# A decode step with expert retrieval: the sample's memory products moved ahead of tile 1's scores, and tile 1's values behind the sample's queries

## The reference

```
xn      = rms_norm(x, g_mix)
q,k,v,gu,gv = split(xn @ w_in)                  # 512, 128, 128, 512, 512 columns
attn    = sink_attention(rope(q), rope(k), v)   # window 128; 8 query heads, 2 key heads
sgu     = gelu(gu) * (tril(w_s) @ rms_norm(gelu(gv)) + b_s)   # per chunk of 128 tokens
x      += concat(rms_norm(attn), rms_norm(sgu)) @ w_out
x      += softmax(q_c @ mem_k / 8) @ mem_v @ w_co,  q_c = rms_norm(x, g_cross) @ w_cq
# experts, for each token and each of 8 heads:
s1, i1  = top_k(q1 @ sub_keys1, 16);  s2, i2 = top_k(q2 @ sub_keys2, 16)
top,sel = top_k(s1[:,None] + s2[None,:], 16);   gate = softmax(top)
idx     = i1*128 + i2 at sel                     # of 16384 experts
x      += sum_k gelu(xn . u_tab[idx_k]) * gate_k * v_tab[idx_k],  xn = rms_norm(x, g_ffn)
y       = rms_norm(x, g_final)
```

## Time and profile before

| | us |
|---|---|
| three runs: median (lowest, highest) | 1709.17 (1706.82, 1710.81) |
| the profiled execution: its own time | 1707.81 |
| its span, first to last instruction | 1706.0 |
| TensorE busy | 1301.5 (76%) |
| VectorE busy | 1165.7 (68%) |
| ScalarE busy | 810.4 (48%) |
| GpSimd busy | 641.3 (38%) |
| data moved | 657.35 MB, mean 385 GB/s |

### The profile page before, as it was taken

How to read it: one execution, slowest core, us unless ns; L and a number is a source line. 1 busy time by engine, 2 the same in 40 slices (tenths; PEclk the granted TensorE clock), 3 DMA queues, 4 the chain that set the end, 5 groups by cost and what they waited for, 6 DMA issues and landing times.

```text
span 1706.0 us, 21619 instructions
## 1 busy us (share of the span) xinstructions
PE 1301.5 (76%) x7069; PEld 475.1 (28%) x7069; DVE 1165.7 (68%) x2795; ACT 810.4 (48%) x2337; POOL 641.3 (38%) x584
## 2 busy tenths in 40 slices
PE   9999878987889776677777776776767677667665
PEld 4455523433444222122322111111111111111110
DVE  2544578887667677787777777777667677677764
ACT  1434366775444354455555454445444445444443
POOL 0000044434434344444444443444444444444441
PEclk9999998899999988899988777878888877888866
DMA  9433699999999999999999999999999999999995
GB/s 353 168 138 134 232 400 422 408 374 422 421 421 421 420 398 420 421 403 421 419 421 412 422 421 421 421 422 421 421 421 421 421 405 422 421 421 420 422 419 220
DMA packets 99041, 657.35 MB, mean 385 GB/s; under 512 B 12576, under 2 KB 17568, under 8 KB 22368
## 3 DMA queue, kind: packets, MB, share of 16 engines
q0 software_dynamic: 83056, 604.28, 85.7%
q1 hardware_dynamic: 15872, 51.68, 8.1%
HBM read 652.71 MB, written 4.19 MB: 385 GB/s over the span
## 4 chain that ended last, share of the span: by engine, by line
DMA 44%; PE 26%; ACT 11%; DVE 10%; issue 7%; POOL 2%; ACTq 0%; DVEq 0%; SPq 0%; POOLq 0%
DMA R<-in_peer_uv,R 43%; PE ps L2009 10%; PE ps L1543 6%; DVE R L1462 4%; PE ps L1802 3%; ACT L911 2%; ACT R L920 2%; PE ps L1515 2%; ACT R L915 1%; POOL R L641 1%; ACT R L911 1%; ACT L826 1%; DVE R L1285 1%; DVE R L1286 1%; DVE R L1288 1%
## 5 line engine op out<-in xcount | busy, mean ns | idle before, releaser
L2009 PE MATMUL ps<-R 64*64 64x512 f32 x4536 | 732.3, 725 | 370.4 <-ACT R L920 364.9
L641 POOL DMA_INDIRECT R<-in_peer_uv,R x567 | 627.8, 1107 | 966.4 <-PE ps L2009 762.8
L1462 DVE CUSTOM_DVE_ANT_0 R<-R 128x1024 f32<-128x1024 f32 x567 | 689.3, 1225 | 382.4 <-DMA R<-in_peer_uv,R 368.3
L911 ACT ACTIVATE R<-R 128x1 f32<-128x1 f32 x576 | 115.9, 201 | 594.6 <-DVE R L1462 585.2
L2009 PEld LDWEIGHTS ps<-R 64*64 64x64 f32 x4536 | 134.5, 149 | 713.3 <-ACT R L920 627.1
L920 ACT ACTIVATE R<-R 128x64 f32<-128x64 f32 x576 | 200.4, 348 | 54.3 <-ACT R L915 1.5
L1802 PE MATMUL ps<-A,R 128*128 128x256 f32 (+1 forms) x640 | 224.8, 479 | 0.7 <-ACT R L802 0.7
L915 ACT ACTIVATE R<-R 128x1 f32<-128x1 f32 x576 | 169.8, 295 | 21.2 <-ACT R L911 0.4
L1802 PEld LDWEIGHTS ps<-A,R 128*128 128x128 f32 (+1 forms) x640 | 96.3, 201 | 261.9 <-issue 260.4
L1543 PE MATMUL ps<-A,R 128*128 128x512 f32 (+1 forms) x256 | 101.1, 547 | 0.0
L911 ACT ACT_TABLE_LOAD x60 | 77.0, 1283 | 9.0 <-DVE R L1462 8.0
(11 more groups left out here) (288 smaller groups left out, 936.6 us busy)
## 6 DMA issues: line engine op xcount, KB each, us to landing
R<-in_peer_uv,R POOLq DMA_INDIRECT x567
A<-in_w_pq SPq DMA_DIRECT2D x8, 1024.0 KB, 10.3
A<-in_w_in SPq DMA_DIRECT2D x3, 2048.0 KB, 20.5
R<-in_w_out SPq DMA_DIRECT2D x5, 1024.0 KB
x_res<-in_x_prompt SPq DMA_DIRECT2D x6, 512.0 KB, 12.9
R<-in_w_out SPq DMA_DIRECT2D x1, 3072.0 KB
R<-in_x_promptT SPq DMA_DIRECT2D x4, 512.0 KB, 9.2
R<-in_w_cq SPq DMA_DIRECT2D x2, 1024.0 KB, 10.9
```

What stands on the lines that cost most here:

```text
L641: pool.indirect_dma_start(slots[slot_of[g]], None, I["peer_uv"][:, :], bass.IndirectOffsetOnAxis(ap=idx[:, b % 4, k:k + 1], axis=0)).then_ ...
L911: act.activation(hgelu[:, b % 2, col], hdot[:, b % 2, col], ACT.Gelu).then_inc(gelu_ready, 1)
L1462: dve.tensor_tensor_reduce(u, u, xn(t), 1.0, 0.0, ALU.mult, ALU.add, hdot[:, b % 2, k:k + 1]).then_inc(u_used, 1)
L2009: ins = pe.matmul(bank(2 * (t % 2) + q)[rows], diag[tokens, g % DIAGS, :], v_rows[slot_of[g]][tokens, c * 512:(c + 1) * 512], start=first, ...
```

## The change

On TensorE's list the memory product (l_pv) moves ahead of tile 1's scores, and both stand after only 4 of the 16 instructions of tile 4's gates, whose rest follows in two pieces behind the fold and behind `half_T(3)`. The transposes of the sample's normed rows move ahead of `gating(4)`; tile 1's value product moves behind `q_mm(0)`, `half_T(4)` behind `scores(0)`, tile 1's transposes behind `q_mm(1)`. On ScalarE the copy of the fold goes ahead of tile 1's exponentials, the sample's norm ahead of tile 4's gates, and the square and root of tile 1's attention behind the sample's score copy. On VectorE tile 1's maxima go behind the sample's weighting, `half_take(3)` and `half_rows(4)` change places, `ffn(0)` signals xn_ready after the lower half (a new semaphore, xn_second, signals the upper one to the first dot product), `attn_scaled(1)` stands behind the first two key searches, and `half_take(4)` and `attn_take(1)` behind `best_pairs(0)`. In the expert loop tile 1's preparation, query, cross, FFN and the first two units start one expert later. Each moved piece keeps its waits, apart from one of VectorE for its own signal attn_out 2, which is left out. No arithmetic is added or removed.

```diff
@@ -351,7 +351,7 @@
...
 
-        xn_ready = sem("xn_ready")
+        xn_ready, xn_second = sem("xn_ready"), sem("xn_second")
         pq_q, pq_qo, pq_t, pq_to, pq_s, pq_so = (sem(n) for n in ("pq_q", "pq_qo", "pq_t", "pq_to", "pq_s", "pq_so"))
@@ -414,11 +414,11 @@
...
 
-        PREP_AT = {1: 1, 2: 122, 3: 200, 4: 210}
-        QUERY_AT = {1: 6, 2: 134, 3: 208, 4: 218}
-        CROSS_AT = {1: 9, 2: 138, 3: 222, 4: 244}
-        FFN_AT = {1: 28, 2: 158, 3: 268, 4: 16 * 23 + 2}
-        UNIT_AT = (24, 31, 38, 44, 51, 57)
+        PREP_AT = {1: 2, 2: 122, 3: 200, 4: 210}
+        QUERY_AT = {1: 7, 2: 134, 3: 208, 4: 218}
+        CROSS_AT = {1: 10, 2: 138, 3: 222, 4: 244}
+        FFN_AT = {1: 29, 2: 158, 3: 268, 4: 16 * 23 + 2}
+        UNIT_AT = (25, 32, 38, 44, 51, 57)
         OUT_AT = (77, 81, 85, 91, 95, 99, 105, 109, 113, 119, 123, 127)
@@ -784,27 +784,22 @@
...
             gating_std(4)
+            act.wait_ge(l_oT, 1)
+            act.activation(oT_c, v3(bank(5)[:, 0:P], 2), ACT.Copy).then_inc(l_oTo, 1)
             act.wait_ge(sc_max, 2)
...
             act.activation(es, es, ACT.Exp).then_inc(sc_exp, 1)
-            act.wait_ge(l_oT, 1)
-            act.activation(oT_c, v3(bank(5)[:, 0:P], 2), ACT.Copy).then_inc(l_oTo, 1)
+            act.wait_ge(x2_out, 1)
+            act.wait_ge(p_tr, 2)
+            row_norm(0, xn(0), f_std, ss_f)
             gates_out(4)
...
             act.activation(pT_one, v3(ps[:, 1024:2048], HEADS), ACT.Copy).then_inc(pT_out, 1)
-
-            act.wait_ge(x2_out, 1)
-            act.wait_ge(p_tr, 2)
-            row_norm(0, xn(0), f_std, ss_f)
             act.wait_ge(f_tr, 1)
...
             half_norm(4)
-            act.wait_ge(attn_out, 2)
-            chain(act.activation(pT_one.rearrange("p a b -> p (a b)")[:, 0:512], o_one, ACT.Square,
-                                 accum_out=ss_a[:, 1:2]))
-            act.activation(ss_a[:, 1:2], ss_a[:, 1:2], ACT.Sqrt, bias=eps[:, 0:1], scale=1.0 / 512).then_inc(n_std, 1)
 
@@ -830,6 +825,10 @@
...
             act.activation(mv_l, mv, ACT.Copy).then_inc(mv_moved, 1)
+            act.wait_ge(attn_out, 2)
+            chain(act.activation(pT_one.rearrange("p a b -> p (a b)")[:, 0:512], o_one, ACT.Square,
+                                 accum_out=ss_a[:, 1:2]))
+            act.activation(ss_a[:, 1:2], ss_a[:, 1:2], ACT.Sqrt, bias=eps[:, 0:1], scale=1.0 / 512).then_inc(n_std, 1)
             queries_out(1)
@@ -1223,13 +1222,6 @@
...
 
-            dve.wait_ge(sc_done, 2)
-            chain(dve.scalar_tensor_tensor(s_one, v3(ps[:, 0:1024], HEADS), 0.125,
-                                           band[:, P:2 * P].unsqueeze(1).broadcast_to([P, HEADS, P]), ALU.mult, ALU.add))
-            chain(dve.tensor_reduce(mx, s_one, AX_X, ALU.max))
-            chain(dve.tensor_tensor(mx, mx, sinks[:, :], ALU.max))
-            chain(dve.tensor_scalar(nmx, mx, -1.0, None, ALU.mult))
-            dve.tensor_tensor(es, nmx, sinks[:, :], ALU.add).then_inc(sc_max, 1)
             dve.wait_ge(l_exp, 1)
@@ -1238,8 +1230,14 @@
...
                               spread[:, 0:8].unsqueeze(2).broadcast_to([P, 8, HD]), ALU.mult).then_inc(l_o, 1)
+            dve.wait_ge(sc_done, 2)
+            chain(dve.scalar_tensor_tensor(s_one, v3(ps[:, 0:1024], HEADS), 0.125,
+                                           band[:, P:2 * P].unsqueeze(1).broadcast_to([P, HEADS, P]), ALU.mult, ALU.add))
+            chain(dve.tensor_reduce(mx, s_one, AX_X, ALU.max))
+            chain(dve.tensor_tensor(mx, mx, sinks[:, :], ALU.max))
+            chain(dve.tensor_scalar(nmx, mx, -1.0, None, ALU.mult))
+            dve.tensor_tensor(es, nmx, sinks[:, :], ALU.add).then_inc(sc_max, 1)
             gating_values(4)
-            half_take(3)
             add_halves(l_wo, x2_out)
@@ -1247,20 +1245,23 @@
...
                 chain(dve.reciprocal(rs_f[r, t:t + 1], ss_f[r, t:t + 1]))
-                for to in (LO, HI) if t == 0 else (ALL,):
-                    ins = dve.scalar_tensor_tensor(xn(t)[to], xr(t)[r], rs_f[r, t:t + 1], g_ffn[r], ALU.mult, ALU.mult)
-                ins.then_inc(xn_ready, 1)
+                dve.scalar_tensor_tensor(xn(t)[r], xr(t)[r], rs_f[r, t:t + 1], g_ffn[r], ALU.mult, ALU.mult)\
+                   .then_inc(xn_ready, 1)
+                if t == 0:
+                    dve.scalar_tensor_tensor(xn(0)[HI], xr(0)[r], rs_f[r, 0:1], g_ffn[r], ALU.mult, ALU.mult)\
+                       .then_inc(xn_second, 1)
 
...
             ffn(0)
+            half_take(3)
             gated(4)
+            half_rows(4)
             dve.wait_ge(pv_done, 2)
...
                               rden.unsqueeze(2).broadcast_to([P, HEADS, HD]), ALU.mult).then_inc(attn_out, 1)
-            half_rows(4)
 
@@ -1273,11 +1274,6 @@
...
                                   ALU.mult).then_inc(n_T, 1)
-
-            dve.wait_ge(attn_out, 2)
-            attn_scaled(1, o_one)
-            half_take(4)
-            attn_take(1)
 
@@ -1331,9 +1327,12 @@
...
                 top_keys(0, c)
+            attn_scaled(1, o_one)
             dve.wait_ge(mv_moved, 1)
...
             best_pairs(0)
+            half_take(4)
+            attn_take(1)
             experts_of(0, 0)
@@ -1453,6 +1452,7 @@
...
                     dve.wait_ge(xn_ready, t + 1)
+                    dve.wait_ge(xn_second, 1)
                 for k in range(TOPK):
@@ -1737,13 +1737,7 @@
...
             project(4, 1)
-            pe.wait_ge(q_out, TILES)
-            pe.wait_ge(kv_out, TILES)
-            for h in (0, 4, 1, 5, 2, 6, 3, 7):
-                rows = slice(64 * (h // 4), 64 * (h // 4) + 64)
-                ins = pe.matmul(ps[:, h * P:(h + 1) * P], qT_one[rows, h % 4, :], kT_of(1)[rows], start=True, stop=True)
-            ins.then_inc(sc_done, 1)
-            project(4, 2, 0, 4)
+            project(4, 2, 0, 2)
             pe.wait_ge(l_pTo, 1)
@@ -1753,19 +1747,25 @@
...
             ins.then_inc(l_pv, 1)
-            project(4, 2, 4, 6)
+            pe.wait_ge(q_out, TILES)
+            pe.wait_ge(kv_out, TILES)
+            for h in (0, 4, 1, 5, 2, 6, 3, 7):
+                rows = slice(64 * (h // 4), 64 * (h // 4) + 64)
+                ins = pe.matmul(ps[:, h * P:(h + 1) * P], qT_one[rows, h % 4, :], kT_of(1)[rows], start=True, stop=True)
+            ins.then_inc(sc_done, 1)
             pe.wait_ge(l_o, 1)
...
             ins.then_inc(l_oT, 1)
-            project(4, 2, 6, KD)
+            project(4, 2, 2, 4)
             pe.wait_ge(l_oTo, 1)
...
             half_T(3)
+            project(4, 2, 4, KD)
             pe.wait_ge(sgu_out, 4)
@@ -1774,15 +1774,10 @@
...
             ins.then_inc(pT_done, 1)
+            pe.wait_ge(xn_ready, 1)
+            sample_T(xn(0), f_tr, False)
             pe.wait_ge(qkT_out, 10)
             gating(4, bank(6))
-            pe.wait_ge(pT_out, 3)
-            for h in range(HEADS):
-                ins = pe.matmul(bank(0)[:, h * HD:(h + 1) * HD], pT_one[:, h, :],
-                                v_rows_of(1)[:, (h // 4) * HD:(h // 4 + 1) * HD], start=True, stop=True)
-            ins.then_inc(pv_done, 1)
-            pe.wait_ge(xn_ready, 1)
-            sample_T(xn(0), f_tr, False)
 
@@ -1832,14 +1827,19 @@
...
             q_mm(0)
-            half_T(4)
+            pe.wait_ge(pT_out, 3)
+            for h in range(HEADS):
+                ins = pe.matmul(bank(0)[:, h * HD:(h + 1) * HD], pT_one[:, h, :],
+                                v_rows_of(1)[:, (h // 4) * HD:(h // 4 + 1) * HD], start=True, stop=True)
+            ins.then_inc(pv_done, 1)
             pe.wait_ge(h_T, 3)
             q_T(0)
-            attn_T(1, o_one, bank(1))
             pe.wait_ge(sgu_out, TILES)
...
             scores(0)
+            half_T(4)
             q_mm(1)
+            attn_T(1, o_one, bank(1))
             pe.wait_ge(n_T, 1)
```

## The result

The changed kernel is slower: 1721.69 us (median of 6 runs, 1716.90 to 1723.17) against 1709.25 us (6 runs, 1706.72 to 1710.81), a ratio of 1.0074, 95% interval 1.0063 to 1.0086. That is 12.4 us where +1.3 was forecast, and above the range.

The account below looks back on a forecast made before the run. The stream of 576 expert gathers bounds the kernel, gated by the first index list and tile 1's output projection end. Projection +3.9, recovery -2.6, other shifts 0: +1.3 us, 1710.5 on the median; range 1704.0 to 1716.5.

Parts of the forecast that it names:

- The other shifts by one expert (query, cross, FFN, first two units) move equal work: 0, within 2 us either way: Expert loop: each ScalarE visit there carries two table loads of 1.28 us, so these shifts cost 0.
- the hole at 371: Gather stream, 371 to 376 us: 3.7 us lost behind the fifth query block's search, unchanged by the change: 0.
- The late projection: Tile 1's output projection waits for both takes, TensorE idles 3.8 us, end +3.9 us, bounds +0.8 and +5.6.
- real gain: Sample's query product on TensorE: idle time gone, takes 3.66 us instead of 6.63, ends 4.5 us earlier.
- the low clock in the projection: Tile 1's output projection: one stretch of 3.4 us at half speed, costing 1.7 us.
- Rival A: Late projection end not absorbed by the stream, clock low for two stretches: +5.6 us, 1714.8 us; chance 0.27.
- The memory wait: TensorE waits 3.8 us for the sample's memory values, whose product then takes 3.4 us; tile 1's exponentials end later.
- The recovery: Gather stream behind the fifth gather: preparation moved off the third expert and a partial refill win back 2.6 of 3.9 us.
- The index list: First index list, which opens the gather stream: ready at 204.85, 0.9 us earlier.
- The table loads: ScalarE table changes: only 1.28 us load, no drain; with the skill's 2.66 us the sum would be +2.7.
- g_ffn: Load for the sample's FFN norm: takes 4.4 us, lands at 180.25, now ends last by 0.5 us.

Follow-up runs that it names:

- e7: Kernel before with only the first two units one expert later (25, 32): 1714.44 us, ratio 1.0030.
- e3: Changed kernel with tile 1's scaling between the two key searches and both takes ahead of the best pairs: 1714.40 us, ratio 1.0034.
- e4: Changed kernel with the memory products behind tile 1's scores again, as before: 1720.30 us, ratio 1.0068.
- e9: Kernel of e5 with the memory products behind tile 1's scores again: 1714.47 us, ratio 1.0036.
- e6: Kernel before with tile 1's preparation, query, cross and FFN one expert later, units unmoved: 1706.93 us, ratio 0.9989.
- e5: Changed kernel with tile 1's scaling and both takes early as in e3, first two units back at 24 and 31: 1711.23 us, ratio 1.0013.
- e15: Kernel of e5 with tile 4's gates ahead of the sample's norm and its gating ahead of the sample's transposes, as before: 1715.56 us, ratio 1.0043.
- e8: Kernel of e6 with xn_ready signalled after the lower half of the scaled rows, no other reordering: 1707.53 us, ratio 0.9994.
- e2: Kernel before with the change's five expert-loop tables (preparation, query, cross, FFN, first two units one expert later): 1711.63 us, ratio 1.0025.
- e12: Kernel of e7 with unit 1's scaling, transposes and take one step earlier: 1712.08 us, ratio 1.0019.
- e13: Kernel before with all six units one expert later, distances between them kept: 1711.90 us, ratio 1.0030.
- e11: Kernel of e9 with tile 4's gates and the copies for the transposes ahead of the sample's norm on ScalarE: 1714.65 us, ratio 1.0035.

## Why the prediction was wrong, step by step

**The failed step is "The other shifts by one expert (query, cross, FFN, first two units) move equal work: 0, within 2 us either way".** The units' shift alone costs 5.1 us in the old order (e7, ratio 1.0030, 1.0017 to 1.0042). The work is equal; its place is not. TensorE at expert 50 waits for VectorE's work at expert 53 instead of 52, and while it stands there, no slot comes free. In the trace of before this wait was visible, 1.81 us at L1971 at 349.27, and the prediction did not look for it: it read the hole at 371 and took the stretch before it as full. The FFN's shift is of the same kind (2.06 us of waiting become 5.65 where the units stay).

**The late projection: mechanism right, size too small.** The forecast had it start 2.9 us later and end 3.9 us later. It started 5.6 and ended 7.5 us later (4.6 and 6.5 without the 0.98 us), beyond the bound of 5.6. It is the larger part of the miss: after the recovery 1.3 us were forecast for it, and undoing the late takes brings 6.8 (e3). Two terms were mis-sized. The "real gain", 4.5 us on the query product, took the full clock for granted; the row of 183 to 190 us has 0.51, after 1.95 us of idle time before the transposes at 182.05, and the scores reached VectorE 0.1 us earlier (1.1 without the 0.98), not 3.0. And the low clock in the projection lasted over 203.3 to about 210 us, which cost 2.5 us, not 1.7. Rival A had named this place, the two stretches and +5.6; the stream's fifth gather was 7.5 us late.

**The memory wait: right in the trace, wrong as a cost.** It is there, 3.54 us before 166.39 and 3.37 us at the low clock as forecast, and it delays the exponentials as forecast. Against the old place of the products it costs nothing (e4, e9), because the sum with w_co's product then comes later by as much or more.

**The recovery: right at gather 9, smaller behind it.** 2.6 us was forecast; gather 5 is 7.5 us late and gather 9 4.8. But gathers 32 to 36 are 7.0 late again and 54 to 57 6.1 to 6.4, so about 1.1 to 1.4 us of the 7.5 came back, and e6 shows too that a lead gained at gather 9 does not last. That gather 9 fits the 2.6 us is no support for the sum.

**The index list**: forecast at 204.85, in the trace 207.43, or 206.45 without the 0.98, so 0.7 us later than before and not 0.9 earlier. **The table loads**: no drain behind them; the root of L722 starts at 179.65, 0.01 us after its load (178.36 + 1.28), so the Trainium skill's 2.66 us a switch ("ScalarE: Activation LUTs", What ACT_TABLE_LOAD costs) again does not show in this kernel, and for this term the row was the better of the two. **g_ffn**: ended last as forecast; VectorE waited for it until 180.55.

The sum in the end, by the ratios: the takes with the clock behind them cost 6.8 us (e3), the units another 3.6 (e5 against e3, with intervals that just overlap; 5.1 in the old order), and 2.2 are left in e5, which makes the 12.6 of the ratio 1.0074. The 1.9 us that the preparation wins (e6) are already in the 2.2: e5 stands 4 us above e6, with intervals that do not meet. Where those 4 us go was not isolated: e15 shows that putting gates and gating back does not win them back.

## What to carry to other kernels

Moving a step by one iteration is not free because the work is the same: look for every wait in which one engine at iteration n needs another's work of iteration n + 2 (or of n - 1, as the transposes that wait for the FFN's copy), and count what one more iteration does to the slots that it holds. When work is moved into a chain to save a few us, check what was standing there idle: the step that now waits (here the projection) pays twice, by the wait and by the clock that falls in it. And a wait that a new order creates is not yet a loss against the old order, even where it stands on the path: compare when the same later point was released in both.

## What the runs showed of the hardware

TensorE's clock fell to 1.2 GHz after idle times of only about 2 us: 1.95 us before 182.05 in the changed kernel was followed by 0.51 over 183 to 190 us, in which it was busy all the time. But not after each: tile 1's scores (L1744, in e8 L1747) follow the same work and the same 2.14 us of waiting in ten traces, and took 1.16 us in five of them (e2, e4, e7, e12, e13), 1.55 and 1.80 in e6 and e8, and 2.07 to 2.08 in before, e9 and e11. A term for the clock behind one short wait therefore differs between executions of the same work. Four matmuls that nobody reads, put into an idle time of 3.6 us, were followed by 2.4 GHz (1.00 instead of 0.57 over 203 to 211 us) and 2.5 us less in the rows behind them. And executions of the same work differ by up to 3.7 us in the first 150 us (L1729's equivalents start between 149.49 and 153.15), before anything that the kernels do differently, so marks in the traces have to be compared from a common point.
